# Reordering the first stage of an encoder layer: z of a tile beside the latents of the tile ahead of it

## What is computed

```
h = rmsnorm(x, norm_mix_g)                 # 1024 wide
p = h @ w_in                               # split by columns:
c_q, c_kv, k_pe = p[:256], p[256:384], p[384:416]        # "latents", 416 columns
z = p[416:2208]                            # 1792 columns, input of the RWKV branch
lat = rmsnorm(c_kv, kv_norm_g);  kpe = rope(k_pe, pos)   # outputs
q = rmsnorm(c_q, q_norm_g) @ w_uq   -> 8 heads of 96, rope, per-head rmsnorm
k, v = lat @ w_ukv (+ kpe)          -> 8 heads, per-head rmsnorm of k
zm = z + (previous row of z - z) * mu      # token shift; first row of a group uses a given row
```

## Time and profile before

| | us |
|---|---|
| median of 3 runs | 1670.44 (1666.98 to 1670.96) |
| the profiled execution, its own time | 1668.39 |
| its span | 1666.2 |
| PE busy | 1510.1 (91%) |
| DVE busy | 861.3 (52%) |
| ACT busy | 445.3 (27%) |
| `inputs_stage` | 0 to 370.4 |
| everything behind it | 370.4 to 1666.2 |

### The profile page before, as it was taken

The page is one execution under the profiler, slowest core; times in us unless marked ns, Lnnn a source line. Parts: engine busy times, 40 slices in busy tenths (PEclk is TensorE's granted clock), DMA queues, the critical chain, the costliest instruction groups (busy, mean ns, idle before and its releaser), DMA issues. The chain is left out here.

```text
span 1666.2 us, 38766 instructions
## 1 busy us (share of the span) xinstructions
PE 1510.1 (91%) x16352; PEld 1070.4 (64%) x16352; DVE 861.3 (52%) x1874; ACT 445.3 (27%) x882; POOL 102.2 (6%) x102
## 2 busy tenths in 40 slices
PE   4999999969999999999998699978997799988894
PEld 2888888854566666666667466644554677766663
DVE  2454555455566676767668476645766233211111
ACT  2222222233222333233231244433453111111110
POOL 0000000000000000000000000000000222332321
PEclk9999999989999999999999699999999799999998
DMA  9332221535142232212122444436754699999972
GB/s 323 137 123 88 94 89 63 191 113 181 58 126 68 80 110 68 80 65 71 50 65 59 108 101 100 101 109 255 276 189 154 227 328 349 344 339 323 324 265 36
DMA packets 101326, 259.55 MB, mean 156 GB/s; under 512 B 34240, under 2 KB 53328, under 8 KB 91824
## 3 DMA queue, kind: packets, MB, share of 16 engines
q1 hardware_dynamic: 93424, 239.92, 42.3%
q0 software_dynamic: 7744, 17.33, 4.5%
HBM read 205.32 MB, written 60.56 MB: 160 GB/s over the span
## 5 line engine op out<-in xcount | busy, mean ns | idle before, releaser
L527 PEld LDWEIGHTS a_ps<-a_hT,a_wz 128*128 128x128 f32 x1792 | 202.6, 192 | 3.8 <-issue 3.8
L527 PE MATMUL a_ps<-a_hT,a_wz 128*128 128x128 f32 x1792 | 204.0, 275 | 0.0
L1918 PE MATMUL d_ps<-late,d_oT 128*128 128x512 f32 x256 | 115.4, 598 | 1.5 <-DVE d_oT L1687 0.8
L2089 DVE COPY f_xT<-f_turned 128x384 f32<-128x384 f32 x32 | 17.9, 558 | 164.9 <-PE f_turned L2056 164.9
L1918 PEld LDWEIGHTS d_ps<-late,d_oT 128*128 128x128 f32 x256 | 46.7, 190 | 51.5 <-issue 50.2
L1453 ACT ACTIVATE late<-c_score,c_top 128x1024 f32<-128x1024 f32 (+8 forms) x72 | 50.6, 703 | 93.2 <-DVE c_top L1402 92.6
L1101 PE MATMUL b_ps<-r_wg,r_hT 128*128 128x512 f32 x128 | 64.9, 640 | 11.5 <-POOL b_S L759 9.7
L2283 DVE TENSOR_SCALAR f_y<-f_down,table 96x512 f32<-96x512 f32 x32 | 23.9, 747 | 98.2 <-PE f_down L2082 98.2
L821 DVE TENSOR_TENSOR b_M<-b_ps,r_causal 128x512 f32<-128x512 f32 x72 | 46.4, 686 | 54.5 <-PE b_ps L1162 54.0
L2082 PE MATMUL f_down<-wd,f_midT 128*96 128x512 f32 x160 | 72.8, 598 | 1.8 <-DVE f_midT L2101 1.8
L2290 ACT ACTIVATE f_xT<-f_turned 128x384 f32<-128x384 f32 x32 | 15.7, 491 | 202.7 <-PE f_turned L2056 202.7
(11 more groups left out here) (363 smaller groups left out, 2847.5 us busy)
## 6 DMA issues: line engine op xcount, KB each, us to landing
wgu<-w_gate_up SPq DMA_DIRECT2D x20, 2048.0 KB
late<-w_gate_up SPq DMA_DIRECT2D x12, 2048.0 KB
wd<-w_down SPq DMA_DIRECT2D x20, 1024.0 KB
late<-w_down SPq DMA_DIRECT2D x12, 1024.0 KB
r_hT<-hT_d SPq DMA_DIRECT2D x18, 512.0 KB, 3.9
b_hT<-hT_d SPq DMA_DIRECT2D x18, 512.0 KB, 4.3
gate_d<-b_logits SPq DMA_DIRECT2D x32, 256.0 KB, 2.6
late<-gate_d SPq DMA_DIRECT2D x8, 1024.0 KB, 5.9
```

The lines of the kernel that those rows point to most:

```text
L527: mm = pe.matmul(banks[Z_BANKS[n % 2]][:, j * P:(j + 1) * P], wz[:, i, (g + j) * P:(g + j + 1) * P], hT[t % 2][:, i, :], start=(i == 0), s ...
L1918: mm = pe.matmul(banks[2 + u][:], oT[t % 2][:, HB * branch(u) + k, :], wo[:, HB * branch(u) + k, half(u)], start=(k == 0), stop=(k == HB - 1))
L2089: copy(xT[b][:, 4 * half:4 * half + 4, :], turned[half][:, 0:4 * CAP].rearrange("p (a b) -> p a b", b=CAP)).then_inc(s[flag], 1)
```

## The change

PE's iteration t now makes z of tile t+1 beside the latents and heads of tile t; z of tile 0 is made ahead of the loop, in between the work on tile PAST, and the last iteration has no z. For this `spread_root`, `normed`, `root_mean` and `square` each run one tile further ahead. The loads come in the order in which the new head of the stage needs them: x, identity, gain and xT of tile 0, then the first z group, and the small constants behind all weights. `shifted(t)` and the store of zm of tile t are in iteration t. `turn_heads(PAST)` moves behind z group 1 of tile 1. Some waits are added where a buffer or PSUM bank is now taken earlier. The diff, cut to its core:

```diff
@@ sync (SP)
+            def load_wz(n):
+                g, k = GROUPS[n]
+                sp.dma_start(wz[:, :, g * P:(g + k) * P], io["w_z"][:, :, g * P:(g + k) * P]).then_inc(wz_in[n], 16)
+
+            load_x(0)
             sp.dma_start(ident[:], io["ident"]).then_inc(first_in, 16)
+            sp.dma_start(g_mix[:], io["norm_mix_g"]).then_inc(first_in, 16)
+            load_xT(0)
+            load_wz(0)
             sp.dma_start(cn[:, QL:], io["past_lat"]).then_inc(past_in, 16)
             sp.dma_start(kpe[:], io["past_kpe"]).then_inc(past_in, 16)
-            load_x(0)
-            load_xT(0)
-            sp.dma_start(g_mix[:], io["norm_mix_g"]).then_inc(first_in, 16)
-            sp.dma_start(wkv[:], io["w_ukv"]).then_inc(first_in, 16)
+            sp.dma_start(wkv[:], io["w_ukv"]).then_inc(wkv_in, 16)
+            load_wz(1)
+            load_x(1)
+            load_xT(1)
+            load_wz(2)
+            sp.dma_start(w[:], io["w_mla"]).then_inc(w_in, 16)
+            load_wz(3)
...
                 sp.dma_start(dst, src).then_inc(consts_in, 16)
-            sp.dma_start(w[:], io["w_mla"]).then_inc(w_in, 16)
-            load_x(1)
-            load_xT(1)
-            for n, (g, k) in enumerate(GROUPS):
-                sp.dma_start(wz[:, :, g * P:(g + k) * P], io["w_z"][:, :, g * P:(g + k) * P]).then_inc(wz_in[n], 16)
-            store_h(0)
             load_x(2)
             load_xT(2)
+            load_x(3)
+            store_h(0)
             store_v(PAST_T)
             store_qk(PAST_T)
+            store_h(1)
+            load_xT(3)
             for t in range(NT):
                 store_latents(t)
-                if t + 1 < NT:
-                    store_h(t + 1)
-                if t + 3 < NT:
-                    load_x(t + 3)
-                    load_xT(t + 3)
-                if t >= 1:
-                    store_zm(t - 1)
+                if t + 2 < NT:
+                    store_h(t + 2)
+                if t + 4 < NT:
+                    load_x(t + 4)
+                    load_xT(t + 4)
+                store_zm(t)
                 store_v(t)
                 store_qk(t)
                 if t == NT - 3:
                     load_for_mixing()
-            store_zm(NT - 1)
@@ vector (DVE)
                     dve.wait_ge(z_done, NG_Z * (t - 1))
+                    dve.wait_ge(p1_done, t - 1)
...
-            dve.wait_ge(first_in, 48)
+            dve.wait_ge(first_in, 32)
             root_mean(0)
             normed(0)
+            dve.wait_ge(past_in, 32)
+            dve.sem_inc(c_ready, 1)
             root_mean(1)
+            normed(1)
             dve.wait_ge(consts_in, 16 * 8)
...
             heads_normed(PAST_T)
             latent_squares(0)
+            root_mean(2)
             for t in range(NT):
                 latents(t)
-                if t + 1 < NT:
-                    normed(t + 1)
-                if t >= 1:
-                    shifted(t - 1)
                 if t + 2 < NT:
-                    root_mean(t + 2)
+                    normed(t + 2)
+                shifted(t)
+                if t + 3 < NT:
+                    root_mean(t + 3)
                 heads_normed(t)
                 if t + 1 < NT:
                     latent_squares(t + 1)
-            shifted(NT - 1)
@@ scalar (ACT): the head of the stage, then the loop
             square(0)
             root(0)
+            copy_z(0, 0)
+            copy_cT(PAST_T)
+            copy_z(0, 1)
             square(1)
             root(1)
-            copy_cT(PAST_T)
             copy_qkv(PAST_T)
+            copy_z(0, 2)
+            copy_z(0, 3)
             head_roots(PAST_T)
             copy_p1(0)
             latent_root(0)
-            copy_turned(PAST_T)
+            square(2)
+            root(2)
...
+            # loop: copy_z(t + 1, n) for copy_z(t, n); square(t + 3), root(t + 3) for t + 2;
+            # copy_turned(PAST_T) in iteration 0, behind copy_z(1, 1)
@@ tensor (PE)
                 if t >= 1:
-                    pe.wait_ge(cT_copied, turn(t - 1))
+                    pe.wait_ge(h_ready, t)
+                    pe.wait_ge(cT_copied, max(t - 1, 1))
...
+                if n == 0:
+                    pe.wait_ge(h_ready, t + 1)
...
                 pe.wait_ge(c_ready, turn(t) + 1)
-                if 0 <= t < NT - 1:
-                    pe.wait_ge(h_ready, t + 2)
+                if t != PAST_T:
+                    pe.wait_ge(h_ready, min(t + 3, NT))
...
             spread_root(0)
-            pe.wait_ge(h_ready, 1)
+            project_z(0, 0)
             turn_latents(PAST_T)
+            project_z(0, 1)
+            pe.wait_ge(wkv_in, 16)
             heads(PAST_T)
+            project_z(0, 2)
+            spread_root(1)
+            project_z(0, 3)
             pe.wait_ge(w_in, 16)
             project(0)
-            turn_heads(PAST_T)
             for t in range(NT):
+                if t + 2 < NT:
+                    spread_root(t + 2)
                 if t + 1 < NT:
-                    spread_root(t + 1)
-                project_z(t, 0)
+                    project_z(t + 1, 0)
                 turn_latents(t)
-                project_z(t, 1)
+                if t + 1 < NT:
+                    project_z(t + 1, 1)
+                if t == 0:
+                    pe.wait_ge(consts_in, 16 * 8)
+                    turn_heads(PAST_T)
                 heads(t)
-                project_z(t, 2)
-                project_z(t, 3)
                 if t + 1 < NT:
+                    project_z(t + 1, 2)
+                    project_z(t + 1, 3)
                     project(t + 1)
                 turn_heads(t)
```

More of the change, by code:

```diff
@@ L173, in inputs_stage @@
         qkT = sb("qkT", [QK, 2 * H, P])
-        (w_in, first_in, past_in, consts_in, ones_set, dve_step,
+        (w_in, wkv_in, first_in, past_in, consts_in, ones_set, dve_step,
          x_squared, r_ms, r_root, r_ready, spread_done, h_ready, z_done, z_copied, zm_ready, row_kept,
@@ L177, in inputs_stage @@
          qk_ready, qkT_done, qkT_copied, lat_stored, v_stored, qk_stored, zm_stored, shift_stored) = (sem(n) for n in (
-             "w_in first_in past_in consts_in ones_set dve_step "
+             "w_in wkv_in first_in past_in consts_in ones_set dve_step "
              "x_squared r_ms r_root r_ready spread_done h_ready z_done z_copied zm_ready row_kept "
@@ L237, in load_for_mixing @@
                 sp.dma_start(early["wg"][0][:], io["w_gates"][:, :, 0:512]).then_inc(early["wg_in0"], 16)
+            def load_wz(n):
+                g, k = GROUPS[n]
+                sp.dma_start(wz[:, :, g * P:(g + k) * P], io["w_z"][:, :, g * P:(g + k) * P]).then_inc(wz_in[n], 16)
+            load_x(0)
             sp.dma_start(ident[:], io["ident"]).then_inc(first_in, 16)
+            sp.dma_start(g_mix[:], io["norm_mix_g"]).then_inc(first_in, 16)
+            load_xT(0)
+            load_wz(0)
             sp.dma_start(cn[:, QL:], io["past_lat"]).then_inc(past_in, 16)
             sp.dma_start(kpe[:], io["past_kpe"]).then_inc(past_in, 16)
-            load_x(0)
-            load_xT(0)
-            sp.dma_start(g_mix[:], io["norm_mix_g"]).then_inc(first_in, 16)
-            sp.dma_start(wkv[:], io["w_ukv"]).then_inc(first_in, 16)
+            sp.dma_start(wkv[:], io["w_ukv"]).then_inc(wkv_in, 16)
[5 more added lines that the diff above has]
+            load_wz(3)
             for dst, src in ((wq[:], io["w_uq"]), (trigs[:], io["trig"].rearrange("t p n -> p t n")),
-                             (mu[:], io["vecs"][:, 0:ZT]), (shift_in[:], io["shift0"]),
                              (g_head[:, 1, :], io["k_head_norm_g"].partition_broadcast(P)),
@@ L250, in _ @@
                              (g_lat[:, 0:QL], io["q_norm_g"].partition_broadcast(P)),
-                             (g_lat[:, QL:], io["kv_norm_g"].partition_broadcast(P))):
+                             (g_lat[:, QL:], io["kv_norm_g"].partition_broadcast(P)),
+                             (mu[:], io["vecs"][:, 0:ZT]), (shift_in[:], io["shift0"])):
                 sp.dma_start(dst, src).then_inc(consts_in, 16)
-            sp.dma_start(w[:], io["w_mla"]).then_inc(w_in, 16)
-            load_x(1)
-            load_xT(1)
-            for n, (g, k) in enumerate(GROUPS):
-                sp.dma_start(wz[:, :, g * P:(g + k) * P], io["w_z"][:, :, g * P:(g + k) * P]).then_inc(wz_in[n], 16)
-            store_h(0)
             load_x(2)
             load_xT(2)
+            load_x(3)
+            store_h(0)
             store_v(PAST_T)
             store_qk(PAST_T)
+            store_h(1)
+            load_xT(3)
             for t in range(NT):
                 store_latents(t)
-                if t + 1 < NT:
-                    store_h(t + 1)
-                if t + 3 < NT:
-                    load_x(t + 3)
-                    load_xT(t + 3)
-                if t >= 1:
-                    store_zm(t - 1)
+                if t + 2 < NT:
[4 more added lines that the diff above has]
+                store_zm(t)
```

(49 more changed lines are left out.)

## The result

The changed kernel took 1673.53 us in the median of 20 runs (1667.8 to 1677.78), the kernel before 1666.76 in 20 runs beside them (1663.48 to 1670.96): ratio 1.0041, 95% interval 1.0031 to 1.0050. It is slower by some 7 us, more than the 0.3% that I had called no change. The profiled execution of the changed kernel took 1674.72 us around a span of 1672.6, against 1668.39 and 1666.2 before: 6.3 us more, where I had forecast 1.3.

What follows compares the result with a forecast made beforehand. PE was taken as the bound, never idle from 36.4 to 333.9 us. Head gains 5.0, an iteration without z is 12.2 shorter, the tail costs 18.5: +1.3 us, forecast 1671.7, range 1665 to 1678.

Steps and rivals of the forecast that it cites:

- The head: Stage start: PE begins z of tile 0 at 12.5; 8.0 gained, 2.0 and 1.0 given back, net 5.0 us.
- The wait: After `project(0)`, PE idles 4.5 us until the diagonal of tile 2 lets the root spread and z of tile 1 start.
- Rival A: Head start kept: no gap opens before z of tile 1; -5.2 us, 1665.2; chance 0.10.
- the hole: The forecast idle stretch of PE after `project(0)`, before the spread of tile 2's root; 4.5 us.
- rival B: Head: constants, loaded behind all weights, come too late for DVE; +3.9, or +6.5 us to 1678; chance 0.10.
- The middle: Loop iterations between head and tail: same instructions, 37.2 us each, the change costs nothing there.
- S: Start of z of tile 8 on PE in the changed kernel, forecast at 316.7; 333.9 before.
- The tail: From S to the next stage, uncovered by z: S + 55.0 against S + 36.5 before, costing 18.5 us.
- `project(8)`: 24.1: Tail: `project(8)` on PE is over 24.1 us after S.
- the 29.2 for the transposes and their copy: Tail: transposes of tile 8's latents and their copy are done 29.2 us after S, then `heads(8)` starts.
- rival C: Tail: clock has fallen by `heads(8)`, whose 4.3 us double; +5.6 us, 1677; chance 0.08.
- the forecast case: Outcome within 5 us of the forecast time 1671.7; chance 0.72.

Runs made afterwards that it cites:

- the first: Changed kernel with the next stage's loads issued one iteration earlier, in iteration 5; ratio to the kernel before 1.0019.
- third experiments: Changed kernel with z of tile 8 made by full-width matmuls in place of narrow ones; ratio to the kernel before 1.0139 (4 runs).
- the fourth: Changed kernel with square and root of tile 2 put ahead of the latents of tile 0 on ACT and DVE; ratio to the kernel before 0.9974.
- fifth: Changed kernel with root of tile 2 ahead of tile 0's latents and next-stage loads one iteration earlier; median 1661.52 us, ratio to before 0.9971.

## Why the prediction was right and wrong

**The head: right, term by term.** PE started at 13.24 (forecast 12.5, bounds 11 to 13.5), with z at half speed at first. `project(0)` ended at 48.6 (47.8). The wait was 4.17 us (4.5), released by the diagonal and made by the order on ACT, as put: with the order turned round it is gone; z of tile 1 started at 53.36 (52.5) and lost 1.2 us (2.0) to the clock. Rival A is refuted, since the hole opened. So is rival B: `project(0)` was followed by the latents' chain at once, and the constants' first user on DVE ran at 40.68 without a wait.

**The middle: right in time.** Iterations took 37.2 us, S was 316.82 (316.7). Nothing was lost or gained there.

**The tail: the step that failed.** I put it at S + 55.0 and it was S + 62.8. That is also outside my own bounds for the next stage, 367 to 377. The failing term is "`project(8)`: 24.1", with the 29.2 for the transposes and their copy, and the heads after it. Up to the last transposes, forecast S + 45.5, it is 53.1, and the 7.6 us are:

- 4.6 up to the end of `project(8)` (345.55 less S is 28.7): the pause of 2.68 and about 1.9 of matmuls at half clock behind it. Moving the loads alone took both away, and putting the loads late into the kernel before brought the pause there.
- 0.4 in the pauses before `heads(8)` (34.2 less 29.2, less 4.6).
- 2.6 from the start of `heads(8)` to the last transposes (18.9 where 16.3 was forecast): the lower clock. This is rival C in mechanism, at 2.6 of the 4.3 us that it put on them, on top of the forecast case instead of in place of it.

The last 9.8 us, from there to the next stage, were forecast as 9.5.

The cause of the first and largest item stood in my own text. "Its first loads are issued in iteration 6 and landed well before; the rest shifts with it" treats the prefetch as something that can only be late. I asked whether its data would be there in time, and not what it would run beside. Before, the 14 loads were issued from 300 to 309.6, under tile 7's z at full width. After, iteration 7 makes the z of tile 8, so the same place in SP's order falls on its 448 narrow matmuls. I had rows for both halves of this, the DMA share and the x128 and x192 of the narrow groups, but no row that showed what such a meeting costs, and did not bound it.

**The sum.** +1.3 forecast, +9.2 in the stage: S was 0.1 off, the rest is the tail's 7.8. The rest of the profiled execution gave 2.8 back, by no cause that I can name; the medians differ by 6.8 us. That the forecast time, 1671.7, is only 1.8 off has luck in it. I added the change to the median of three runs, 1670.44, and the kernel before has a median of 1666.76 in twenty. From there the same sum gives 1668.0, and the miss is the 5.5 us by which +1.3 falls short of +6.8. The times given for rivals B and C were also added up wrongly: their +6.5 and +5.6 hold the 1.3 of the sum already, so from 1670.4 they come to 1677 and 1676, not 1678 and 1677. The stated range of 1665 to 1678 held the time, while the chance of 0.16 for slower was too small: A, B and C were all priced from the head and the clock, and what the tail's own transfers might cost had no price.

**What stays open.** Why `heads(8)` runs at the lower clock in the changed kernel and in the first and third experiments but not in the fourth and fifth, behind nearly the same pauses. Why the wide form of z for tile 8 costs another 5 to 11 us in stages that it does not touch. And whether 0.3% is the end: the head gives some 6 us by its order alone, and with z moved the same 5 come out by another way; the two were not combined further.

## What to carry to other kernels

Work that is moved ahead shortens the iterations behind it, and every transfer that hangs on an iteration's number slides with it: ask of each prefetch not only when it lands but which instructions it now runs beside, above all where many short ones use up the instruction stream. Work at the end of a loop that looks like a plain cost may be the cover of the last tile's chain; here 25 us of z moved to the head gained 5 there and cost 18.5 at the end by plain arithmetic, of which the shorter iteration gave back 12.2. And when a loop begins one tile ahead, read the queue of each helper engine for what stands in front of the first thing the loop needs: the root of one tile put ahead of the latents of another took 6 us from this stage.

## What the runs showed that I had not expected

PE can stand still with every semaphore set and all data there. With the DMA engines filled by loads (0.93 to 1.06 in the windows of the changed kernel) and narrow matmuls running, the packet of instructions that the kernel with early loads gets 14 to 15 us behind S came 17 to 20 us behind it, and PE stood for 1.57 to 2.68 us in three kernels. Asked for by tenths of a microsecond, the three late packets stand at 336.1 (the changed kernel), 350.1 (the kernel before with late loads) and 327.7 (the root ahead), and PE resumes at 338.52, 352.50 and 330.15: 2.4 us behind the packet each time, however long it had stood. That ties the packet to PE, which its row does not name. The profile marks the pause "issue"; the line of the instruction queue in the DMA view is what shows its cause. The matmuls behind the pause also run at the lower clock: 15 of them took 7.20 us in the changed kernel, where 16 take 5.75 at full speed, and 7.19 behind the pause of only 1.57.
